# Turning heads inside the context attention, modulation pieces placed earlier, six early gathers instead of four

## The reference

```python
for i in range(2):
    mx, mc = modulation(c, w_mod[i], b_mod[i]), modulation(c_ctx, w_mod[i], b_mod[i])   # six vectors of 1024 each
    hx = modulate(rmsnorm(x, norm1[i]), mx[0], mx[1])
    hc = modulate(rmsnorm(h, norm1[i]), mc[0], mc[1])
    ox, oc = mix_even(...) if i == 0 else mix_odd(...)        # attention groups; h is the context stream
    x = x + mx[2] * ox
    x = x + mx[5] * peer(modulate(rmsnorm(x, norm2[i]), mx[3], mx[4]), ...)
    if i == 0:
        h = h + mc[2] * oc
        h = h + mc[5] * peer(modulate(rmsnorm(h, norm2[i]), mc[3], mc[4]), ...)
```

## Time and profile before

| what | us |
|---|---|
| median of 3 runs | 4426.19 (4411.77 to 4430.12) |
| the profiled execution, its own time | 4407.58 |
| span of that execution, first to last instruction | 4406.3 |
| busy in it: PE / DVE / ACT / POOL | 3757.3 / 2603.1 / 1746.1 / 1689.1 |
| bytes moved | 1562.74 MB, 355 GB/s over the span |
| from the span's start to the turning block's first matmul | 285.7 |
| first expert block / second expert block | 519.2 to 2567 / 3050.7 to 4406.3 |

### The profile page before, as it was taken

The page is one execution under the profiler, slowest core; times in us unless marked ns, Lnnn a source line. Parts: engine busy times, 40 slices in busy tenths (PEclk is TensorE's granted clock), DMA queues, the critical chain, the costliest instruction groups (busy, mean ns, idle before and its releaser), DMA issues. The chain is left out here.

```text
span 4406.3 us, 44443 instructions
## 1 busy us (share of the span) xinstructions
PE 3757.3 (85%) x12678; PEld 1911.6 (43%) x12678; DVE 2603.1 (59%) x5667; ACT 1746.1 (40%) x5137; POOL 1689.1 (38%) x1350
## 2 busy tenths in 40 slices
PE   5988789899998899878999966787989997877787
PEld 2444644555554445433444422556444552222222
DVE  3524687667866855676644433436766558666554
ACT  1112255555554444443333322322664433333333
POOL 0100144444444443444545412001444534656665
PEclk9989999999999999999999987899999999999999
DMA  4255899999999999999999971028999999999998
GB/s 174 108 212 198 288 424 401 412 419 424 404 425 426 426 420 426 427 391 427 427 427 427 427 295 37 4 86 297 394 372 412 425 423 405 427 427 427 427 427 363
DMA packets 248572, 1562.74 MB, mean 355 GB/s; under 512 B 30851, under 2 KB 44963, under 8 KB 77190
## 3 DMA queue, kind: packets, MB, share of 16 engines
q0 software_dynamic: 185088, 1342.36, 73.1%
q1 hardware_dynamic: 61014, 213.99, 12.9%
q10 hardware_dynamic: 2224, 3.55, 0.2%
HBM read 1551.43 MB, written 8.36 MB: 354 GB/s over the span
## 5 line engine op out<-in xcount | busy, mean ns | idle before, releaser
L2823 PE MATMUL ps<-ring,ex_diag 128*128 128x512 f32 x5120 | 2476.7, 618 | 416.6 <-ACT ex_diag L2812 389.7
L1586 POOL DMA_INDIRECT ring<-in_p_uv,expert x1280 | 1633.8, 1276 | 2179.3 <-PE ps L2823 1447.4
L2787 DVE SCALAR_TENSOR_TENSOR ring<-ring,H 128x1024 f32<-128x1024 f32 x1280 | 1557.5, 1225 | 1084.0 <-DMA ring<-in_p_uv,expert 1041.2
L2823 PEld LDWEIGHTS ps<-ring,ex_diag 128*128 128x128 f32 x5120 | 923.9, 194 | 1663.6 <-ACT ex_diag L2812 847.5
L2806 ACT ACTIVATE ex_act_w<-ex_dots 128x1 f32<-128x1 f32 x1280 | 258.1, 202 | 1471.4 <-DVE ring L2787 1465.2
L2812 ACT ACTIVATE ex_diag<-ident_sb,ex_weight 128x128 f32<-128x128 f32 x1280 | 513.9, 402 | 91.6 <-issue 3.1
L2808 ACT ACTIVATE ex_weight<-ex_act_w,gates 128x1 f32<-128x1 f32 x1280 | 377.1, 295 | 91.3 <-issue 4.2
L532 PE MATMUL ps<-win_w,hT 128*128 128x512 f32 (+1 forms) x480 | 191.9, 557 | 1.9 <-PEq L283 1.4
L532 PEld LDWEIGHTS ps<-win_w,hT 128*128 128x128 f32 x480 | 90.3, 191 | 106.0 <-issue 103.9
L1945 PEld LDWEIGHTS ps<-hTc,bs_w 128*128 128x128 f32 x768 | 110.8, 191 | 29.3 <-issue 23.5
L1945 PE MATMUL ps<-hTc,bs_w 128*128 128x128 f32 (+1 forms) x768 | 120.3, 310 | 0.3 <-issue 0.3
(11 more groups left out here) (456 smaller groups left out, 3314.6 us busy)
## 6 DMA issues: line engine op xcount, KB each, us to landing
ring<-in_p_wqk SPq DMA_DIRECT2D x64, 576.0 KB, 4.8
bs_w<-in_p_wqk SPq DMA_DIRECT2D x64, 576.0 KB, 8.0
ca_mod_w<-in_w_mod SPq DMA_DIRECT2D x24, 1024.0 KB, 9.5
ring<-in_p_uv,expert POOLq DMA_INDIRECT x1280, 13.9
win_mod_w<-in_w_mod SPq DMA_DIRECT2D x16, 1024.0 KB, 4.8
bs_w<-in_e_w_out_tiles SPq DMA_DIRECT2D x24, 512.0 KB, 8.0
win_w<-in_e_w_in SPq DMA_DIRECT2D x9, 1024.0 KB, 8.9
mod_mod_w<-in_w_mod SPq DMA_DIRECT2D x8, 1024.0 KB, 14.8
```

Of the source, the lines that this page charges most:

```text
L1586: pool.indirect_dma_start(m.ring[:, r, :], None, a["p_uv"], bass.IndirectOffsetOnAxis(ap=m.expert[:, t % 2, slot % SLOTS:slot % SLOTS + 1] ...
L2787: dve.scalar_tensor_tensor(out=ring[:, r, 0:D], in0=ring[:, r, 0:D], scalar=1.0, in1=h_of(t + t0), op0=ALU.mult, op1=ALU.mult, accum_out=d ...
L2823: mm = pe.matmul(mix_banks(t)[:, half, :], diag[:, b, :], ring[:, r, D + half * BANK:D + (half + 1) * BANK], start=(n == 0), stop=(n == SL ...
```

## The change

Four edits:

- **Turning.** The block `turn_heads` is gone. A class `Turns` takes its place inside the context attention: the 8 parts of the two context tiles are turned at the start of the block, through 8 banks, before anything else; the 16 parts of the four latent tiles are turned one by one at slots 3, 9, 15, ... 93, all through one bank (bank 1), and copied back by ScalarE two slots later.
- **Banks of the modulation** in the context attention: one (bank 0) in place of two. The first piece of the second and third group of 8 pieces so waits until VectorE has taken the group before it.
- **Places of the modulation pieces.** In `project_heads` the 16 pieces follow units 10 to 25 instead of 14 to 29. In the context attention the 24 pieces are spread over the first 88 of the 102 slots.
- **Early gathers.** `EARLY` is 6. The ring of query weights has three places in ring buffers 6 and 7, and the fourth in memory of its own.

```diff
@@ class Modulation
-        if k == 0 and g >= 2:
-            pe.wait_ge(self.row_ready, self.COLS * (g - 1))
+        if k == 0 and g >= len(self.banks):
+            pe.wait_ge(self.row_ready, self.COLS * (g - len(self.banks) + 1))
         for j in range(self.COLS):
-            mm = pe.matmul(self.m.ps[32 * j:32 * j + 2, self.banks[g % 2], :], self.m.csil[:, k, 2:4],
+            mm = pe.matmul(self.m.ps[32 * j:32 * j + 2, self.banks[g % len(self.banks)], :], self.m.csil[:, k, 2:4],
@@ project_heads
-    MOD_AT = NU - mods.pieces
+    MOD_AT = NU - mods.pieces - 4
@@
-def turn_heads(nc, m):
...
+class Turns:
+    def __init__(self, m, s, bank):
+        self.m, self.bank = m, bank
+        heads = lambda t: [(m.KV[:, t, KA:KA + 512], 4), (m.KV[:, t, KB:KB + P], 1)] \
+            + [(q_of(m, t)[:, c * BANK:(c + 1) * BANK], 4) for c in range(2)]
+        self.first = [part for t in range(CT) for part in heads(t)]
+        self.rest = [part for t in range(CT, NT) for part in heads(t)]
...
+        for n in range(len(self.rest)):
+            self.at["turn"].put(3 + 6 * n, n)
+            self.at["copy"].put(5 + 6 * n, n)
...
+    def begin_tensor(self, pe):
+        for n, part in enumerate(self.first):
+            self.turn(pe, part, n).then_inc(self.turned, 1)
+        for q in range(2):
+            pe.wait_ge(self.copied[q], len(self.first) // 2)
...
+    def tensor(self, pe, slot):
+        for n in self.at["turn"](slot):
+            if n:
+                pe.wait_ge(self.rest_copied, n)
+            self.turn(pe, self.rest[n], self.bank).then_inc(self.rest_turned, 1)
+
+    def scalar(self, act, slot):
+        for n in self.at["copy"](slot):
+            x, blocks = self.rest[n]
+            act.wait_ge(self.rest_turned, n + 1)
+            act.copy(x, self.m.ps[:, self.bank, 0:blocks * P]).then_inc(self.rest_copied, 1)
@@ context_attention
-        mods = Modulation(m, a, s, 1, [0, 1, 2], 8, (0, 1))
+        mods, turns = Modulation(m, a, s, 1, [0, 1, 2], 8, (0,)), Turns(m, s, 1)
...
-        steps = [slots * n // mods.pieces for n in range(mods.pieces)]
+        steps = [(slots - 14) * n // mods.pieces for n in range(mods.pieces)]
...
+                turns.begin_tensor(pe)
                 for slot in range(slots):
...
+                    turns.tensor(pe, slot)
@@
-EARLY = 4
+EARLY = 6
@@ first_choice
-        w_o = m.ring[:, 0:EARLY, :].rearrange("p r d -> p (r d)").rearrange("p (k d) -> p k d", d=D)
-        w_q = m.ring[:, EARLY:, :].rearrange("p r d -> p (r d)")[:, 0:RING * (KC + 1) * P].rearrange("p (r d) -> p r d", r=RING)
+        w_o = m.ring[:, 0:KC // 2, :].rearrange("p r d -> p (r d)").rearrange("p (k d) -> p k d", d=D)
+        behind = m.ring[:, EARLY:, :].rearrange("p r d -> p (r d)")
+        w_q = [behind[:, r * (KC + 1) * P:(r + 1) * (KC + 1) * P] for r in range(RING - 1)] + [s.sb("w_q", [P, (KC + 1) * P])]
```

49 lines of the change are left out of this document (20 added, 29 removed).

## The result

The changed kernel takes 4390.42 us (median of 8 runs, 4383.95 to 4394.74). The kernel before, run beside it, takes 4413.51 (8 runs, 4405.55 to 4430.12). The ratio is 0.9948, 95% interval 0.9934 to 0.9962, which is 17 to 29 us. The forecast said 15.2 us less, but a time of 4411.0 in a range from 4396, and that range does not hold 4390.42. One thing has to be known to read this: in about one execution of five the kernel before takes 4424 to 4434 us and in the others at most 4419, and two of the three runs shown before the prediction (4426.19 and 4430.12) were of the first sort.

A forecast was written before the change was run, and what follows sets the result against it. The expert blocks were taken as bound by DMA, so gains lie ahead of them: -17.1 + 4.5 + 3.0 - 5.8 + 0.2 = -15.2 us. That gave 4392.4 like the profiled execution, 4411.0 carried to the median; range 4396 to 4428.

The forecast's parts named there:

- the sum: All terms together: -17.1 + 4.5 + 3.0 - 5.8 + 0.2 = -15.2 us, with no change of clock counted.
- The signs that the prediction names in the trace: First piece near 285 us, short TensorE idle, two addition waits, six gathers then POOL idle 13 us, first expert instruction 509.
- End of the projection to the first piece: From TensorE's projection end to the context attention's first piece: 285.0 instead of 302.07, so -17.1 us (-17.5 to -15).
- Turned parts inside: Sixteen turned parts inside the context attention cost TensorE +4.5 us (+1 to +8.5); ScalarE's copies cost nothing.
- One bank: In the context attention TensorE must wait twice for VectorE's four additions: +3.0 us (0 to +6).
- The attention as a whole: Context attention from first piece to last product: 7.5 us longer, from turned parts and waits for additions.
- End of the attention: At the context attention's end, rows stored earlier leave less behind the last product: -5.8 us (-6.2 to -5).
- Early gathers: Start of both expert blocks: barrier opens 5.1 us later with 5.1 us more gathered, 0 each (-2.3 to +1.5).
- Rival 1: TensorE's clock stays up through the attention's first 20 us: up to 7.6 us less, -22.8 in all, 4403; chance 0.17.
- Rival 2: At the expert blocks the barrier does not wait for the gathers: -19.8 us in all, 4406; chance 0.08.
- Rival 3: Nothing comes out: attention terms at upper ends, each expert block loses 1.5 us or more: -5, 4421; chance 0.13.
- Rival 4: Slower: in the attention TensorE waits at bank 1's 15 hand-overs for ScalarE's copies: +28 us, 4454; chance 0.04.

The follow-up runs named there:

- run 1: The kernel before with only the projection's 16 modulation pieces placed four units earlier: 4396.39 us, 0.9963 of before.
- run 12: The kernel before with only the projection's 16 pieces four units earlier, timed once more on another chip: 4395.14 us, 0.9963 of before.
- run 5: The changed kernel with all 24 parts turned ahead of the first piece, through 8 banks, none inside the attention: 4388.56 us, 0.9951 of before.
- run 9: The kernel of run 5 (all parts turned first) with two banks for the modulation pieces in place of one: 4385.89 us, 0.9941 of before.
- run 2: The kernel before with only the early gathers raised from four to six: 4409.77 us, ratio 1.0; its profiled execution took 4436.63 us.
- run 3: The changed kernel with four early gathers in place of six: 4390.86 us, 0.9958 of before.
- run 4: The changed kernel again with no edit: 4393.12 us, 0.9955 of before; its profiled execution took 4404.47 us.
- run 10: The kernel of run 9 with the attention's 24 pieces over 96 slots in place of 88: 4391.37 us, 0.9957 of before.
- run 6: The changed kernel with the attention's 24 pieces over 96 slots in place of 88: 4384.72 us in 4 runs, 0.9935 of before.
- run 7: The changed kernel with VectorE's four additions two slots earlier: 4398.54 us, 0.9972 of before.
- run 11: The changed kernel with the projection's pieces back after units 14 to 29: 4397.8 us, 0.9965 of before.

## Why the prediction was right and wrong

**The step that failed** is the last one of the sum: "That execution was faster than all three runs, whose median is 4426.19; the difference is carried over to it: 4411.0." Beside the twelve kernels the same program had medians of 4409.62, 4410.74 and 4410.73 us. In the result it is 4413.51. So the level was 13 to 16 us too high, and the range was hung on it: begun at 4413.51 in place of 4426, it would start at 4384 and hold 4390.42. Of the 20.6 us between 4411.0 and 4390.42, 12.7 are the level and 7.9 are gain beyond the sum (23.1 measured for 15.2). The profiled 4407.58 was an ordinary execution, and two of the three runs shown were long ones; the 4392.4 that the prediction names for an execution like the profiled one was the better forecast. Three runs of 4411.77, 4426.19 and 4430.12, with a profile at 4407.58, could be read as two groups. I read one spread out of them. The signs that the prediction names in the trace came nearly all as written, while its time did not.

**End of the projection to the first piece**, forecast -17.1 (-17.5 to -15). Measured 283.81 against 302.07, -18.3; by the other profiles of either kernel 284.67 and 304.61, -19.9. Both lie outside the bounds, on the good side. The chain was as written: 0.71 us of idle time before the first transpose, SP's first load at 278.93 where I had 280.2, 4.88 us from there to the piece where I had 4.77. SP was 1.3 us quicker than my count of semaphores said. Runs 1 and 12 show that the pieces' earlier places alone are worth 6.8 to 10.7 at the first gather.

**Turned parts inside**, forecast +4.5 (+1 to +8.5). Run 5 takes them out: 5.4 us from the change's shortest attention, 8.4 to 8.6 from the two others. That is no clean measure of the term, because run 5 also has the clock at 1.00 at the start; how much of it is the parts stays open. Much of the parts does fall into waits, as I took: the waits for ScalarE are 4.7 us shorter than in run 5 (4.3 + 0.5 against 6.9 + 2.6, the same there as in run 9). A part of four blocks takes 0.53 us at full clock (304.02 to the next instruction at 304.55), and three of the twelve ran at half, one of them 0.99 us (371.13 to 372.12); I had priced all at 0.46.

**One bank**, forecast +3.0 (0 to +6): two waits of 0.96 and 2.02 us in the trace, 3.0 together. What they cost in the end is less sure; run 9 removes them and gains 0.2 us in its one profile, with a lower clock against it, so that any value from 0 to 3 is open.

**The attention as a whole** was forecast 7.5 us longer. It is 6.6 to 9.8 longer in the three profiles with the change's attention (92.1, 95.1, 95.3 against 85.5).

**End of the attention**, forecast -5.8: 0.80 us from the last product to the next block where 6.76 were, so -5.96.

**Early gathers**, forecast 0: runs 2 and 3, ratio 1.0 (0.9985 to 1.0015, which is 7 us either way) for that edit alone. The barrier waits for the landing: POOL's idle time grew by 4.0 and 1.5 us, for 5.1 forecast, the first expert instruction came at 508.06 for 509, and the DMA engines were empty for 4 to 5 us as before. The second seam grew less than the first, which the forecast did not have.

**The sum**, forecast -15.2. First gather: 487.20, 491.58 and 491.85 in the profiles with the whole lead of the change, 504.89 and 505.87 before; the means differ by 15.2 us. That the figure is hit to the tenth is luck: on the same means the first piece comes 18.9 us earlier (17.1 forecast), the attention is 8.5 longer (7.5), and from the last product to the first gather it is 4.8 shorter (5.8 less 0.2). The medians differ by 23.1 and 16.5. What they have beyond 15 is no term of mine: a few microseconds lie behind the first gather in the first profile, as in runs 1 and 12, but none in that of run 4, and their cause is open.

**Rival 1, the clock.** It came half, and was given back. The attention's early stretch is at 0.99 from 296 to 340, and its end from 364 on is at 0.50, where before was at 1.00; the mean over the attention is 0.86, and 0.88 before. The rival's price of 7.6 us comes near what run 10 shows: with the 400 matmuls that the attention had before, it takes 78.5 us at 1.00 throughout, 7.1 less than the 85.5 of before. Its start depends on what stands ahead. In the three kernels that turn all parts first, TensorE works through to the first piece with 0.83 us idle, and all three profiles have 1.00 from 280 to 330. In five profiles with the idle time of about 3 us (the change twice, runs 3, 6 and 7) the clock fell to the lower level behind it. Run 11 lies between: over 1.53 us ahead of the first piece it stayed at 1.00, and it fell behind a second wait, of 1.36 us before 294.90. Its end goes with the pieces: 0.50 in the seven profiles where they stop at slot 84, 1.00 in the seven where they go on. Runs 6 and 10 moved them and nothing else, against the change and run 9; the sum had no term for it. The Trainium skill's page TensorE: Matmul & The Clock Gate ("What's actually happening") has the throttled state as the default that activity releases. These profiles agree with it at the start of the attention. They also show that a TensorE which the profile has as busy can stay at the lower level: 0.50 with 7.94 of 8 us busy in the change (286 to 294), and with 44.30 of 46 in run 2 (358 to 404).

**Rival 2** (no wait for the gathers) fell with the 14.29 us. **Rival 3** (nothing comes out) fell with the interval of the ratio. **Rival 4** (hand-over of bank 1) did not come: no wait for a copied part is among TensorE's waits.

## What to carry to other kernels

- Before a difference is carried over to a median of few runs, ask whether the runs are of one kind: where a profile is faster than all of them, forecast from the profile's own time, and put the other level into the range. This cost 12.7 us here, more than any term of the sum was off.
- Time at the end of a block is cheap to win: what stands behind the last matmul (an addition, a store that is waited for) was 13 us at two seams, and moving its source a few units earlier took it out. But look at what its source did where it stood: the attention's end lost its full clock with the pieces. Work put ahead of a barrier gained nothing measurable here, where the barrier waits until it has landed.
- Pure waiting of TensorE can hide small parts, but only at the clock that it has there. Moving a wait's releaser ahead on a shared engine (run 7) moved the wait to the next one behind it.

## What the runs showed of the hardware

From one execution to the next the clock of TensorE can move more than the edits do. The same attention program took 85.5 us and, in run 2's profile, 111.4. With the parts ahead and two banks, it took 86.5 us with the clock at 0.66 from 330 to 350 and 0.53 at its end, and 78.5, with the pieces in other slots, at 1.00 throughout. The falls inside the attention that I followed stand behind waits of TensorE of 0.7 to 4.4 us, and yet the same wait of 1.60 us was followed by a fall in run 9 and by none in runs 5 and 10. I had not expected a program whose executions fall into two groups 20 us apart, as those of the kernel before do, nor that one of its edits, the pieces four units earlier, would come with none of the long group in 21 runs. The 7.53 us of idle time that it removes are not enough to make one: run 11 has them too and none of the long group in 12 runs. What makes them stays open.
